# DeltaNet heads: parameters, decay differences and exponentials of the next head made in the tail of the current one

## The reference

```python
G = jnp.cumsum(gc, axis=-1)                                  # gc: log of the decay, per token
decay = jnp.exp(jnp.where(tri, G[..., :, None] - G[..., None, :], -jnp.inf))
lmat = jnp.where(strict, bc[..., :, None] * einsum('bhik,bhjk->bhij', kc, kc) * decay, 0.0)
eg = jnp.exp(G)
rhs = bc[..., None] * (vc - eg[..., None] * einsum('bhck,bhkv->bhcv', kc, S))
u = triangular_solve(eye + lmat, rhs, lower=True, unit_diagonal=True)
o = eg[..., None] * einsum('bhck,bhkv->bhcv', qc, S) + einsum(
    'bhij,bhjv->bhiv', einsum('bhik,bhjk->bhij', qc, kc) * decay, u)
tail = jnp.exp(G[..., -1:] - G)
S_new = jnp.exp(G[..., -1])[..., None, None] * S + einsum('bhck,bhcv->bhkv', kc * tail[..., None], u)
```

## Time and profile before

| | |
|---|---|
| Median of 3 runs | 4041.88 us (4040.19 to 4042.7) |
| The profiled execution | 4042.75 us, span 4041.1 us |
| TensorE (PE) busy | 3807.0 us, 94% of the span |
| TensorE weight loads (PEld) busy | 2931.7 us, 73% |
| VectorE (DVE) busy | 1802.4 us, 45% |
| ScalarE (ACT) busy | 943.6 us, 23% |
| GpSimd (POOL) busy | 1207.4 us, 30% |
| DMA | 223.99 MB, mean 55 GB/s |
| Granted TensorE clock, mean | 0.975 |

### The profile page before, as it was taken

How to read it: one execution, slowest core, us unless ns; L and a number is a source line. 1 busy time by engine, 2 the same in 40 slices (tenths; PEclk the granted TensorE clock), 3 DMA queues, 4 the chain that set the end, 5 groups by cost and what they waited for, 6 DMA issues and landing times. The chain is left out here.

```text
span 4041.1 us, 54777 instructions
## 1 busy us (share of the span) xinstructions
PE 3807.0 (94%) x20290; PEld 2931.7 (73%) x20290; DVE 1802.4 (45%) x2980; ACT 943.6 (23%) x2138; POOL 1207.4 (30%) x1021
## 2 busy tenths in 40 slices
PE   8999999998899999999999888989979999999999
PEld 5666666666677888878867766666657688887887
DVE  4565556655443111136661226666655411112666
ACT  3333332333210000000001015555631100000001
POOL 0111011111142333323331106656633233332432
PEclk9999999998699999999999999999989999999999
DMA  4111011111231111123332220000033111112322
GB/s 149 33 38 38 27 34 36 38 38 27 72 98 54 42 42 42 42 88 103 92 121 59 68 74 2 1 2 1 1 95 94 66 42 42 42 42 64 109 86 80
DMA packets 322017, 223.99 MB, mean 55 GB/s; under 512 B 28442, under 2 KB 313235, under 8 KB 319827
## 3 DMA queue, kind: packets, MB, share of 16 engines
q1 hardware_dynamic: 316164, 214.99, 18.0%
q0 software_dynamic: 2048, 5.25, 0.5%
q10 hardware_dynamic: 3650, 1.64, 0.2%
HBM read 191.54 MB, written 34.37 MB: 56 GB/s over the span
## 5 line engine op out<-in xcount | busy, mean ns | idle before, releaser
L775 PE MATMUL ps<-xT,work 128*128 128x272 f32 x2688 | 643.4, 392 | 0.0
L775 PEld LDWEIGHTS ps<-xT,work 128*128 128x128 f32 x2688 | 510.7, 190 | 105.3
L1320 PE MATMUL ps<-xn,work 128*128 128x363 f32 (+1 forms) x1536 | 547.2, 475 | 6.8 <-issue 6.7
L775 PE MATMUL ps<-xn,work 128*128 128x272 f32 x2016 | 489.9, 392 | 3.9 <-DVE work L846 3.9
L775 PEld LDWEIGHTS ps<-xn,work 128*128 128x128 f32 x2016 | 382.9, 190 | 83.9 <-issue 5.1
L387 PE MATMUL ps<-work 128*128 128x272 f32 x1676 | 404.3, 398 | 13.4 <-PEq L1155 7.3
L387 PEld LDWEIGHTS ps<-work 128*128 128x128 f32 x1676 | 321.8, 193 | 84.3 <-issue 17.2
L2946 POOL TENSOR_SCALAR work<-work 128x640 f32<-128x640 f32 (+4 forms) x192 | 313.6, 1643 | 196.7 <-DVE work L2849 196.4
L1320 PEld LDWEIGHTS ps<-xn,work 128*128 128x128 f32 x1536 | 260.7, 191 | 105.5 <-issue 21.4
L648 POOL TENSOR_TENSOR xT<-xT,work 128x272 f32<-128x272 f32 x96 | 198.3, 2078 | 253.2 <-DVE work L512 164.4
L2032 POOL TENSOR_TENSOR xT<-xT,consts 128x512 f32<-128x512 f32 x96 | 127.6, 1336 | 451.9 <-DVEq L1859 391.3
(11 more groups left out here) (425 smaller groups left out, 5841.4 us busy)
## 6 DMA issues: line engine op xcount, KB each, us to landing
work<-in_ffn_w_in_dram SPq DMA_DIRECT2D x88, 512.0 KB, 5.1
xn<-in_ffn_w_out_dram SPq DMA_DIRECT2D x46, 704.0 KB, 4.5
work<-in_gdn_w_in_dram SPq DMA_DIRECT2D x32, 512.0 KB, 4.2
work<-in_ffn_w_out_dram SPq DMA_DIRECT2D x18, 704.0 KB, 4.5
ffn_parked_residual<-xT SPq DMA_DIRECT2D x2, 4352.0 KB, 13.7
work<-in_gdn_w_out_dram SPq DMA_DIRECT2D x32, 256.0 KB, 2.8
work<-in_nsa_w_out_dram SPq DMA_DIRECT2D x64, 128.0 KB, 2.9
xT<-ffn_parked_residual SPq DMA_DIRECT2D x4, 1632.0 KB, 10.2
```

Source lines behind the costliest of these rows:

```text
L775: ins = pe.matmul(acc(a, n), w[:, k, :], t[:, k, a * SUB:(a + 1) * SUB], start=(first and k == 0), stop=(k == HK - 1), skip_group_check=True)
L1320: mm = pe.matmul(unit_acc(u, m), w[j % 2][:, k, :], c.xn[:, k, o:o + cnt], start=(k == 0), stop=(k == KD - 1))
```

## The change

A new function `differences(n, settle, first)` on VectorE holds the parameter copy and the decay differences of head n. It is called for head 0 in the code ahead of the loop and for head i + 1 in the tail of head i, after the first `normed` and before the wait for L1688. It first waits for a new semaphore, `du`, which TensorE raises with the product L1417, and L1417 is moved ahead of the eight products of L1415. A new function `decays(n)` on ScalarE holds the two exponentials (first `e2`, then `eg`). It is called for head 0 ahead of the loop and for head i + 1 right behind L1690, ahead of the last take of the projection and of the logarithm. The tap copy to `cw` moves from the start of a head to the second level, behind L1908. No instruction of work is added or left out; `TURNED`, the count of VectorE's chained steps that the last head lacks, goes from 10 to 12 accordingly.

```diff
@@ -1150,8 +1150,9 @@
             "scales_spread", "tile_normed", "conv_rows_turned", "conv_kept", "gate_product", "gate_product_kept", "zeroed", "gates_turned",
             "gate_vector_step", "gate_scalar_step", "gate_sums", "gate_rows_turned", "gate_rows_kept", "gate_rows_stored")
         ctr, cev = sems(nc, ctx, c, "conv_group_turned", "conv_group_kept")
-        (oc, osq, oss, ort, yd, dc, pc, first_step) = sems(
-            nc, ctx, c, "o_copied", "o_squared", "o_summed", "o_rooted", "y_done", "vector_chain", "params_copied", "first_conv_chain")
+        (oc, osq, oss, ort, yd, dc, pc, first_step, du) = sems(
+            nc, ctx, c, "o_copied", "o_squared", "o_summed", "o_rooted", "y_done", "vector_chain", "params_copied", "first_conv_chain",
+            "decays_used")
         with nc.Block() as block:
             @block.sync
             def _(sp):
@@ -1411,10 +1412,10 @@
                     pe.wait_ge(str_, i * 8 + 8)
                     alone()
                     pe.matmul(c.ps[:, S:S + NS], us2_[0:NS, :], blk(e2, gs, 0), start=True, stop=False, skip_group_check=True)
+                    pe.matmul(c.ps[:, Dp:Dp + NB], par(LOGA, 8, NS).to_broadcast([NS, P]), const(c, "batch_s")[0:NS, :], start=True, stop=True).then_inc(du, 1)
                     for b in range(NB):
                         pe.matmul(c.ps[:, S + TS * b:S + TS * b + TS], s0[:, b * P:(b + 1) * P],
                                   qT[:, TP + TS * b:TP + TS * b + TS], start=False, stop=(b == NB - 1), skip_group_check=True)
-                    pe.matmul(c.ps[:, Dp:Dp + NB], par(LOGA, 8, NS).to_broadcast([NS, P]), const(c, "batch_s")[0:NS, :], start=True, stop=True)
                     pe.wait_ge(um2, i + 1)
                     for hf in range(2):
                         mm = pe.matmul(c.ps[:, A + 512 * hf:A + 512 * hf + 512], tok(kt, gs, 0), um[0:NS, 512 * hf:512 * hf + 512],
@@ -1628,6 +1629,13 @@
                     act.wait_ge(taken, n * UNITS_A_HEAD + (U_SQ, U_SK)[j] + 3)
                     act.activation(rq[j], rq[j], ACT.Exp, scale=-0.5).then_inc(rooted, 1)
 
+                def decays(n):
+                    act.wait_ge(gl, n * 32 + 32)
+                    act.wait_ge(e2d, n + 1)
+                    act.activation(e2, e2, ACT.Exp).then_inc(e2r, 1)
+                    act.wait_ge(pc, n + 1)
+                    act.activation(eg, gb, ACT.Exp).then_inc(egr, 1)
+
                 def head(i, more):
                     n = i + 1
                     events = [(E[m], lambda j=j, m=m: take_unit(n, j, m, False)) for j, E in ((0, E_Q), (1, E_K), (2, E_V), (3, E_Z)) for m in range(3)]
@@ -1637,11 +1645,6 @@
                     events += [(E[m], lambda j=j, m=m: log(n, j, m)) for j, E in ((0, E_SQ), (1, E_SK)) for m in range(3)]
                     events += [(E_SK[2] + 1, lambda: root(n, 1)), (E_SK[2] + 2, lambda: root(n, 0))]
                     turn = Turn(events, more)
-                    act.wait_ge(gl, i * 32 + 32)
-                    act.wait_ge(pc, i + 1)
-                    act.activation(eg, gb, ACT.Exp).then_inc(egr, 1)
-                    act.wait_ge(e2d, i + 1)
-                    act.activation(e2, e2, ACT.Exp).then_inc(e2r, 1)
                     for gi, g in enumerate(PAIR):
                         turn.before("p1", gi)
                         act.wait_ge(p1, i * 2 + gi + 1)
@@ -1688,6 +1691,8 @@
                     act.activation(eb, c.ps[:, Dp:Dp + NB], ACT.Exp).then_inc(oc2, 1)
                     act.activation(osq_[:, TP:NT], c.ps[:, S:S + NS], ACT.Square)
                     act.activation(oS[:, TP:NT], c.ps[:, S:S + NS], ACT.Copy).then_inc(osq, 1)
+                    if more:
+                        decays(i + 1)
                     turn.before("oss")
                     act.wait_ge(oss, i + 1)
                     for o, cnt, acc in proj_parts(c, 3):
@@ -1722,6 +1727,7 @@
                 for j in (1, 0):
                     root(0, j)
                 take_unit(0, 3, 2, True)
+                decays(0)
                 with act.Fori(0, HG - 1) as i:
                     head(i, True)
                 head(HG - 1, False)
@@ -1800,7 +1806,7 @@
                     dve.tensor_copy(gate_out[0:72, :], bank(c, 4)[0:72, 0:2 * P]).then_inc(rk, 1)
                     dve.wait_ge(a1g, 6)
                 CHAIN = 37
-                TURNED = 10
+                TURNED = 12
 
                 def conv_tap(n, j, t, settle, first=False):
 
@@ -1828,26 +1834,27 @@
                     dve.wait_ge(rooted, n * 2 + 2 - j)
                     dve.tensor_tensor((qT, kT)[j], nxt[j], rq[j], ALU.mult).then_inc(kq, 1)
 
-                def head(i, more):
-                    n_chain = [0]
-
-                    def settle(ins):
-
-                        n_chain[0] += 1
-                        ins.then_inc(dc, 1)
-                        dve.wait_ge(dc, i * CHAIN + n_chain[0])
-
-                    turn = Turn([(TAPS[j][t], lambda j=j, t=t: conv_tap(i + 1, j, t, settle)) for j in range(3) for t in range(4)], more)
-                    settle(dve.tensor_copy(parh, c.par[:, ds(i * NPAR, NPAR)]))
+                def differences(n, settle, first=False):
+                    if not first:
+                        dve.wait_ge(du, n)
+                    settle(dve.tensor_copy(parh, c.par[:, ds(n * NPAR, NPAR)]))
                     dve.sem_inc(pc, 1)
-                    if more:
-                        dve.wait_ge(conv, i * 3 + 3)
-                        settle(dve.tensor_copy(cw, c.convw[:, ds(i + 1, 89)][:, 0:89:8]))
-                    dve.wait_ge(gl, i * 32 + 32)
+                    dve.wait_ge(gl, n * 32 + 32)
                     for g in PAIR:
                         dve.tensor_tensor(grp(e2, g), grp(gb, g), parg(GCUM, g).to_broadcast([P, 4, P]), ALU.subtract)
                     settle(dve.tensor_scalar(e2[:, TP:NT], gb[:, TP:NT], par(GCUM, 8, P), None, ALU.subtract))
                     dve.tensor_scalar(e2, e2, 0.0, None, ALU.min).then_inc(e2d, 1)
+
+                def head(i, more):
+                    n_chain = [0]
+
+                    def settle(ins):
+
+                        n_chain[0] += 1
+                        ins.then_inc(dc, 1)
+                        dve.wait_ge(dc, i * CHAIN + n_chain[0])
+
+                    turn = Turn([(TAPS[j][t], lambda j=j, t=t: conv_tap(i + 1, j, t, settle)) for j in range(3) for t in range(4)], more)
                     for gi, g in enumerate(PAIR):
                         turn.before("p1", gi)
                         dve.wait_ge(p1, i * 2 + gi + 1)
@@ -1906,6 +1913,9 @@
                             dve.transpose(blk(x, gs, 0), blk(xt, gs, 0)).then_inc(sxrd, 1)
                             settle(dve.tensor_tensor(blk(e2, gs, 0), blk(e2, gs, 0), const(c, "upper_s")[0:NS, :], ALU.mult))
                             dve.tensor_tensor(blk(e2, gs, 0), ps(gs.Y, gs, 0), blk(e2, gs, 0), ALU.mult).then_inc(sx, 1)
+                            if more:
+                                dve.wait_ge(conv, i * 3 + 3)
+                                settle(dve.tensor_copy(cw, c.convw[:, ds(i + 1, 89)][:, 0:89:8]))
                         elif l in (2, 3):
                             turn.before("sY", l - 2)
                             dve.wait_ge(syr, i * 2 + l - 1)
@@ -1951,6 +1961,7 @@
                     turn.before("o2")
                     if more:
                         normed(i + 1, 1)
+                        differences(i + 1, settle)
                     dve.wait_ge(oc2, i + 1)
                     for b in range(NB):
                         ins = dve.scalar_tensor_tensor(out=sn[:, b * P:(b + 1) * P], in0=s0[:, b * P:(b + 1) * P], scalar=eb[:, b:b + 1],
@@ -1991,6 +2002,7 @@
                         conv_tap(0, j, t, settle_first, first=True)
                 normed(0, 1)
                 normed(0, 0)
+                differences(0, settle_first, True)
                 with dve.Fori(0, HG - 1) as i:
                     head(i, True)
                 head(HG - 1, False)
```

More of the change, by code:

```diff
@@ L1829, in normed @@
                     dve.tensor_tensor((qT, kT)[j], nxt[j], rq[j], ALU.mult).then_inc(kq, 1)
+                def differences(n, settle, first=False):
+                    if not first:
+                        dve.wait_ge(du, n)
+                    settle(dve.tensor_copy(parh, c.par[:, ds(n * NPAR, NPAR)]))
+                    dve.sem_inc(pc, 1)
+                    dve.wait_ge(gl, n * 32 + 32)
+                    for g in PAIR:
+                        dve.tensor_tensor(grp(e2, g), grp(gb, g), parg(GCUM, g).to_broadcast([P, 4, P]), ALU.subtract)
+                    settle(dve.tensor_scalar(e2[:, TP:NT], gb[:, TP:NT], par(GCUM, 8, P), None, ALU.subtract))
+                    dve.tensor_scalar(e2, e2, 0.0, None, ALU.min).then_inc(e2d, 1)
                 def head(i, more):
@@ L1840, in head @@
                     turn = Turn([(TAPS[j][t], lambda j=j, t=t: conv_tap(i + 1, j, t, settle)) for j in range(3) for t in range(4)], more)
```

(10 more changed lines are left out.)

## The result

The changed kernel took 4019.42 us (median of 5 runs, 4017.53 to 4023.93); the kernel before, on the same chip, 4042.7 us (4040.19 to 4045.08). The ratio is 0.9943, with a 95% interval of 0.9929 to 0.9958: 23.3 us less, where 16.6 us were forecast. The profiled execution of the changed kernel took 4019.42 us with a span of 4017.8 us, against 4042.75 and 4041.1 before.

The account below looks back on a forecast made before the run. TensorE was taken as the bound, so only its stalls count: 6.1 + 6.8 + 3.7 = 16.6 us off 4042.75 gives 4026.2, and 4025.3 us as median; range 4016 to 4034.

Parts of the forecast that it names:

- Both waits go: Heads 2 to 7: TensorE's waits at L1373 and the first L1385 vanish, worth 6.1 and 6.8 us.
- VectorE's new work lies in its idle gap: Head's tail: differences run from 224.6 to about 227.3, 1.2 us before ScalarE releases L1956, and cost nothing.
- The lower bound: Wait for L1417 in the tail: its signal comes quickly, so L1956 is delayed by nothing; upper bound 2.5 us.
- The root 1.5 us later, and harmless: ScalarE's tail: exponentials delay root L1696 by 1.5 us, unmoved at low clock; TensorE has 1.3 us in hand.
- only half: Rival: root a further 1.3 us later, L1385's wait mostly returns, gain 8.0 us, time 4033.9 us; chance 0.07.
- The drain of a table load: ScalarE's tail: the skill's drain of about 1.38 us per table load was taken as absent from the trace.
- Nothing for the tap copy: Second level of the head: moving the tap copy there was counted as no gain, at most 0.4 us a head.
- The last head: No filling there, so VectorE's chain is TensorE's; L1857 starts sooner, 3.7 us gained, root unmoved at low clock.
- The clock neutral: TensorE's tails: number of low-clock tails is a draw whose mean does not move, so 0 us from the clock.
- a better clock: Rival: only two of the seven boundaries at low clock, some 8 us less, 4017 us; chance 0.08.

Follow-up runs that it names:

- late-signal kernel: Changed kernel with the moved product L1417 put back behind the eight state products, the semaphore still on it: 4022.17 us, ratio 0.9952.
- the pair with the denser tail: Next head's filling products spread one at a time between the tail's narrow products, on the kernel before (4027.84 us, 0.9961) and on the changed kernel (4015.74 us, 0.9927).
- the longer head: Changed kernel with three filling products added at the start of each of seven looped heads, 1.83 us a head: 4040.3 us, ratio 0.9992.

## Why the prediction was right, and where its sum was off

- **Both waits go: right.** 12.3 us against 12.9. Part of the 0.6 us between them is that the shown wait of L1373 is longer behind a low tail (0.9 to 1.0 us against 0.6); where the clock stays up there is less to win.
- **VectorE's new work lies in its idle gap: right.** Forecast: done at 227.3, 1.2 us ahead of L1956's release. Measured: done at 227.52, and 1.25 us still waited. The signal took 0.16 us. The lower bound was the right one, and the late-signal kernel shows the price if it isn't: 0.69 us a head for 0.64 us of lateness.
- **The root 1.5 us later, and harmless: right.** 1.44 us where the boundary is at full clock. At the last boundary, which has a low tail, it does not move, as forecast: L1975 starts 3.98 us after the head's first L1361, L1964 started 3.97 after it. Moving the exponentials out of its way gained nothing in the heads, so the rival "only half" falls, and more widely: another order has 1.4 us more room and is worth nothing to TensorE in the looped heads.
- **The drain of a table load: not there.** The load of 231.33 ends at 232.61 and L1699 starts at 232.63. The Trainium skill (ScalarE: Activation LUTs, What ACT_TABLE_LOAD costs) would put some 1.4 us of drain there; the trace of this boundary has no room for it.
- **Nothing for the tap copy: right in the sum, for a better reason than mine.** Alone it gains some 3 us, but it gains them from the same chain as the rest; with the whole change the chain is no longer late.
- **The last head: right in mechanism, mis-sized.** Forecast 3.7 us, measured 6.3. L1864 starts 6.70 us after the head's first L1361, where L1857 started after 10.49: 3.8, the forecast's term. A further 1.1 us is in VectorE's twelve steps from there to L1386, 11.70 us before and 10.56 after: three of them were lengthened beside GpSimd's work before, two are now (last section). The last 1.3 us come further on in the head. In the pair with the denser tail the sum of 3.7 us is met by luck: there the boundary is at full clock, so the exponentials do delay the root, the chain starts only 2.35 us sooner (8.06 us after the first L1361 instead of 10.41), and the same 1.1 us of VectorE's steps makes up for it. VectorE in the changed kernel, whose last head begins at 960.68:

```profile
967.38 0.68 DVE L1864 TENSOR_TENSOR xT<-ps,xT 128x512 f32<-128x512 f32 x1
```

In the two with the denser tail, the changed kernel (its last head begins at 960.62) and the kernel before (967.09):

```profile
968.68 0.68 DVE L1866 TENSOR_TENSOR xT<-ps,xT 128x512 f32<-128x512 f32 x1
```

```profile
977.50 0.69 DVE L1859 TENSOR_TENSOR xT<-ps,xT 128x512 f32<-128x512 f32 x1 [1.23 <-ACT xT L1646]
```

- **The clock neutral: wrong.** This is the failed term. The forecast let the low tails stand as they were and gave 8% to a better clock, worked out as 4017 us. Its eight us came true in size (7.9): not by two low tails instead of five, as it was worked out, but by one of 6.8 us and three of 3.4. The 5.9 us between forecast and result would have been some 9 but for the rest of the span, which took 3 us more. The Trainium skill (TensorE: Matmul & The Clock Gate, What's actually happening) has the chip's observation run freely of the kernel. What I drew from it, that the number of low tails is a draw whose mean doesn't move, did not hold: with the narrow tail as it was, 17.0 us in all four profiles with a head of 120.4 us, 30.6 or more in all five with a head of 121.13 us or above, and the longer head brought them back with the tail untouched. A clock observed freely of the kernel is not refuted by this.
- **The rest of the kernel**, in which nothing was changed, took 3.1 us more in this pair of profiles. It moved between 2945 and 2954 us over the profiles of this study, and it moved with the low-clock time inside it: 2945 to 2948 us with 91 to 94 us at the lower level, 2950 to 2951 with 97 to 101, 2953 to 2954 with 104 to 111. By this, in this pair, the clock that gave 7.9 us in the heads took about 3 back here. Why it falls there more often in one profile than in another is not known.

What is not settled: why a head of 120.4 us has fewer low tails than one of 121.1 or 122.3. That a change outside the tail brings the low clock back is shown by one experiment; it adds dense products at the head's start to do so, and whether these or the length by itself brought the low tails back was not separated. A third reading was not tested: if the chip decides at times of its own, the head's length sets how the next tail meets them, and then one length is good and another bad without shorter being better. That filling products spread through a narrow tail keep the clock up is shown on the kernel before, where no low tail is left; in the changed kernel one low tail of 13.7 us stayed, and why it stayed in the fourth head is open.

## What to carry to other kernels

Work that an engine does ahead of the chain that others wait for is worth at most its length, and once, however many waits hang on that chain (0.4 to 0.5 us a head for the tap copy alone): find its idle gap one stage earlier, and there check the cover of what it is put ahead of. If TensorE's granted clock falls in some repetitions of a stage and not in others, count the low time per kernel before and after, since a shorter loop can gain or lose by it as much as by the waits (here 7.9 us beside 12.3). And where such a tail is made of narrow products, try to spread the dense ones through it, but leave one behind the last narrow product if another engine's latency hides there.

## What the runs showed of the hardware that was not expected

- Reordering alone, with the same products, took 14 us from the kernel before (4042.14 to 4027.84): its low tails vanished.
- Low-clock time can repeat to the tenth: 17.0 us in four profiles out of four of the two kernels with the changed one's head length and tail; 13.7 us in the same head on two chips. It need not: 30.6 and 43.8 us in two profiles of the kernel before.
- Within one kernel the time follows the granted clock: the changed kernel with the denser tail took 4010.14 us at a mean clock of 0.980, 4017.69 at 0.977 and 4020.89 at 0.976.
- VectorE's two-input products of 128x512 elements take 0.69 us by themselves and 1.6 to 1.8 us when they start while a GpSimd operation runs. Two that start within 0.01 us of GpSimd's (246.00 and 974.26 in the changed kernel) keep their 0.69 us, and GpSimd's own then took 1.83 us at 246.00, where it had taken 1.28 at 240.67. In the changed kernel's last head (VectorE in order of time, then GpSimd's pair from 974.25) two of the four such products are of the long kind, 2.1 us more than they need; in the kernel before it was three of four:

```profile
968.94 1.80 DVE L1867 TENSOR_TENSOR xT<-xT,consts 128x512 f32<-128x512 f32 x1 [0.15 <-DVE xT L1865]
970.78 0.69 DVE L1868 TENSOR_TENSOR xT<-consts,xT 128x512 f32<-128x512 f32 x1
...
974.26 0.69 DVE L1867 TENSOR_TENSOR xT<-xT,consts 128x512 f32<-128x512 f32 x1
974.99 1.64 DVE L1868 TENSOR_TENSOR xT<-consts,xT 128x512 f32<-128x512 f32 x1
```

```profile
974.25 3.50 POOL L2044 TENSOR_TENSOR xT<-xT,consts 128x512 f32<-128x512 f32 x2 [4.05 <-DVEq L1866]
```
